# RWKV triangular inverses: from whole 64x64 blocks to 32x32 blocks with a corner, and where projection products stand

## The reference

```python
def step(s, inp):
    r_t, w_t, k_t, v_t, kk_t, a_t = inp
    sa = jnp.einsum('bhvk,bhk->bhv', s, -kk_t)
    s = (s * w_t[:, :, None, :] + sa[..., None] * (kk_t * a_t)[:, :, None, :]
         + v_t[..., None] * k_t[:, :, None, :])
    return s, jnp.einsum('bhvk,bhk->bhv', s, r_t)
```

## Time and profile before

| | us |
|---|---|
| median of 3 runs | 4723.03 |
| lowest and highest of them | 4722.28, 4724.2 |
| the profiled execution | 4724.49 |
| its span, first to last instruction | 4722.8 |

### The profile page before, as it was taken

One profiled execution on the slowest core, in us unless ns is written; L12 is line 12 of the kernel. 1 busy time (PEld: TensorE's weight loads), 2 busy tenths in 40 slices (PEclk: granted clock), 3 DMA queues, 4 the chain that ended last, 5 costly groups with the idle time before them and its releaser, 6 DMA issues. The chain is left out here.

```text
span 4722.8 us, 86694 instructions
## 1 busy us (share of the span) xinstructions
PE 4354.9 (92%) x40017; PEld 2726.9 (58%) x40017; DVE 1375.2 (29%) x2899; ACT 539.0 (11%) x1016; POOL 134.1 (3%) x253
## 2 busy tenths in 40 slices
PE   5899999999999999799999987999995999999995
PEld 2577768686868776677777764554442333333331
DVE  1133333424142524324444552110123111111112
ACT  1011212112111211200111000000010000000001
POOL 0000000000000000100000000000000000000000
PEclk7899999999999999899999988999997999999997
DMA  9111111111111111121122106875128999999997
GB/s 357 47 57 34 48 34 49 44 44 48 37 48 35 48 37 39 53 64 54 55 60 62 51 6 224 295 258 198 62 81 319 372 390 391 396 398 390 387 395 288
DMA packets 412717, 738.32 MB, mean 156 GB/s; under 512 B 16382, under 2 KB 255300, under 8 KB 389444
## 3 DMA queue, kind: packets, MB, share of 16 engines
q1 hardware_dynamic: 405060, 697.65, 41.1%
q0 software_dynamic: 7296, 35.13, 2.7%
HBM read 689.21 MB, written 43.52 MB: 155 GB/s over the span
## 5 line engine op out<-in xcount | busy, mean ns | idle before, releaser
L512 PE MATMUL psR<-hT,wrkv 128*128 128x320 f32 x3584 | 983.0, 435 | 16.5 <-DMA wrkv<-in_w_in 16.5
L512 PEld LDWEIGHTS psR<-hT,wrkv 128*128 128x128 f32 x3584 | 683.3, 191 | 300.7 <-DMA wrkv<-in_w_in 17.0
L992 PE MATMUL psH<-hT,whg 128*128 128x320 f32 x2560 | 706.2, 434 | 24.4 <-DMA whg<-in_w_in 24.4
L992 PEld LDWEIGHTS psH<-hT,whg 128*128 128x128 f32 x2560 | 482.7, 191 | 215.9 <-DMA whg<-in_w_in 24.9
L526 PE MATMUL psR<-X 64*64 64x64 f32 x8960 | 285.7, 220 | 8.3 <-ACT X L715 3.7
L1277 PE MATMUL psM<-branches,wmg 128*128 128x512 f32 x512 | 265.1, 600 | 23.9 <-DMA branches<-outr_scratch 22.7
L526 PEld LDWEIGHTS psR<-X 64*64 64x64 f32 x8960 | 271.8, 135 | 24.6 <-ACT X L715 9.7
L1451 PE MATMUL psO<-wout,mergedT 128*128 128x512 f32 x480 | 208.7, 597 | 6.3 <-DMA wout<-in_w_out 5.8
L822 DVE TENSOR_TENSOR X<-X,psR 128x256 f32<-128x256 f32 (+1 forms) x240 | 90.6, 377 | 382.3 <-PE psR L526 380.5
L1837 DVE SCALAR_TENSOR_TENSOR hid<-hid,psE 128x512 f32<-128x512 f32 x16 | 11.0, 688 | 586.9 <-ACT hid L1797 586.9
L1716 PE MATMUL psE<-hT,xg 128*32 128x512 f32 x1392 | 168.6, 603 | 3.2 <-DMA hT<-in_moe_w_gate 2.6
(11 more groups left out here) (345 smaller groups left out, 4726.5 us busy)
## 6 DMA issues: line engine op xcount, KB each, us to landing
hT<-in_ada_w SPq DMA_DIRECT2D x64, 1024.0 KB, 8.3
wrkv<-in_w_in SPq DMA_DIRECT2D x56, 1024.0 KB, 6.0
mergedT<-in_moe_w_down SPq DMA_DIRECT2D x46, 1024.0 KB, 20.9
hT<-in_moe_w_gate SPq DMA_DIRECT2D x45, 1024.0 KB, 19.0
wmore<-in_moe_w_up SPq DMA_DIRECT2D x44, 1024.0 KB, 21.1
hT<-in_moe_w_down SPq DMA_DIRECT2D x43, 1024.0 KB, 22.3
hT<-in_moe_w_up SPq DMA_DIRECT2D x42, 1024.0 KB, 19.2
mergedT<-in_moe_w_up SPq DMA_DIRECT2D x42, 1024.0 KB, 19.4
```

The costliest lines, as they stand in the source:

```text
L512: mm = nc.tensor.matmul(ps[:, 2 * (n % 2) + h, 0:HALF], w[:, n % SLOTS, k, :], S["hT"][:, k, h * HALF:(h + 1) * HALF], start=(k == 0), sto ...
L992: mm = nc.tensor.matmul(ps[:, b + h, 0:HALF], w[:, i, k, :], S["hT"][:, k, h * HALF:(h + 1) * HALF], start=(k == 0), stop=(k == KT - 1))
```

## The change

The inverse of a 64x64 triangular matrix is taken by 32x32 blocks. The two diagonal blocks of each head are inverted by the same doubling, in 5 levels, with four 32x32 matmuls (`blocks`) where two of 64x64 stood. The off-diagonal block is then one step: the off-diagonal block of N times one diagonal inverse, a turn of the other, a copy into YT, and a product (the corner). POOL and DVE put the blocks into a new tile TI, which the scan reads. The chunk groups of the inverse are two of 5 chunks (HALVES) in place of 4, 4 and 2, so a level has 4 units. G1 and G3 are still whole 64x64 grams; the diagonal blocks are taken out by quarters (32 partitions each): G1's by DVE with a mask, G3's by ACT, with the off-diagonal block (Noff), and POOL applies the mask to G3's. `fill(42)` ahead of the inverse and 48 of the `fill(52)` behind it move: four products behind each of the 20 units, five more behind the last unit, five behind the off-diagonal step; four remain ahead of the scan. ACT takes gate tiles 2 and 3 ahead of its copies of units 2 and 11. `make_masks` makes four 64-wide masks in place of six and three 32-wide ones (cd: two strict triangles of -1, and the identity).

The diff, cut to its core:

```diff
-        X = [sb(f"X{d}", [P, NCH, 3, L]) for d in both]
+        X = [sb(f"X{d}", [P, NCH, 3, BL]) for d in both]
+        Noff = [sb(f"Noff{d}", [P, NCH, BL]) for d in both]
+        TI = [sb(f"TI{d}", [P, NCH, L]) for d in both]
+        YT = X[0]
...
-        UNITS, LEV = len(GROUPS), 6
+        HALVES = ((0, 5), (5, 5))
+        UNITS, LEV = len(HALVES), 5
+        near = [[slice(L * h + BL * d, L * h + BL * d + BL) for h in range(2)] for d in both]
+        far = [near[1 - d] for d in both]
...
         def _(pool):
+            for d in both:
+                nc.gpsimd.memset(TI[d][:, :, :], 0.0).then_inc(sem("ti_zeroed"), 1)
+            pool.wait_ge(sem("ti_zeroed"), 2)
...
-                        pool.wait_ge(sem("m_ready"), (2 * r + d) * 3 + g + 1)
-                        nc.gpsimd.tensor_tensor(X[d][:, c0:c0 + n, 2, :], X[d][:, c0:c0 + n, 1, :], bcast(ci[:, :], n, 1), ALU.add)\
+                        pool.wait_ge(sem("m_ready"), 4 * ((2 * r + d) * 3 + g + 1))
+                        nc.gpsimd.tensor_tensor(X[d][:, c0:c0 + n, 2, :], X[d][:, c0:c0 + n, 1, :], bcast(cd[:, 2, :], n, 1), ALU.add)\
+                            .then_inc(sem("tt_begun"), 1)
+                        pool.wait_ge(sem("g3_taken"), 6 * ((2 * r + d) * 3 + g + 1))
+                        nc.gpsimd.tensor_tensor(X[d][:, c0:c0 + n, 0, :], X[d][:, c0:c0 + n, 0, :], bcast(cd[:, 1 - d, :], n, 1), ALU.mult)\
                             .then_inc(sem("tt_begun"), 1)
                 for i in range(2, 4):
                     store_gate(i)
+                pool.wait_ge(sem("inv_added"), INV * (r + 1))
+                for d in both:
+                    for i in range(4):
+                        q, at = slice(BL * i, BL * i + BL), BL * (i % 2)
+                        nc.gpsimd.tensor_copy(TI[d][q, :, at:at + BL], X[d][q, :, 2, :]).then_inc(sem("ti_diag"), 1)
...
+            def blocks(out, lhsT, rhs):
+                for i in range(4):
+                    q = slice(BL * i, BL * i + BL)
+                    mm = nc.tensor.matmul(out[q], lhsT[q], rhs[q], start=True, stop=True)
+                return mm
...
                 for i in range(LEV):
                     for d in both:
-                        for k, (c0, n) in enumerate(GROUPS):
+                        for k, (c0, n) in enumerate(HALVES):
                             q = (i * 2 + d) * UNITS + k
                             if q >= 2:
                                 W("inv_copied", inv_copied(r, q - 2))
                                 if inv_added(r, q - 2) > r * INV:
                                     W("inv_added", inv_added(r, q - 2))
+                            if i >= 2:
+                                W("inv_added", inv_added(r, q - 2 * UNITS))
                             for c in range(c0, c0 + n):
...
                                 if i < LEV - 1:
-                                    mm = heads(o[:, 0:L], M, N)
+                                    mm = blocks(o[:, 0:BL], M, N)
                                 if i < LEV - 2:
-                                    mm = heads(o[:, L:P], N, M)
+                                    mm = blocks(o[:, BL:L], N, M)
                                 if i:
-                                    mm = heads(t, N, TT)
+                                    mm = blocks(t, N, TT)
                             mm.then_inc(sem("inv_sums"), 1)
-
-            def scan(r):
+                            fill(4)
+                fill(5)
                 W("inv_copied", INV * (r + 1))
                 W("inv_added", INV * (r + 1))
+                for k, (c0, n) in enumerate(HALVES):
+                    y, t = cols(4 + 2 * k, n, BL), cols(5 + 2 * k, n, BL)
+                    for c in range(c0, c0 + n):
+                        for d in both:
+                            for h in range(2):
+                                nc.tensor.matmul(y[near[d][h], c - c0, :], Noff[d][far[d][h], c, :], X[d][far[d][h], c, 2, :],
+                                                 start=True, stop=True)
+                        for d in both:
+                            for h in range(2):
+                                mm = nc.tensor.matmul(t[near[d][h], c - c0, :], X[d][near[d][h], c, 2, :], cd[near[d][h], 2, :],
+                                                      start=True, stop=True)
+                    mm.then_inc(sem("far_sums"), 1)
+                fill(5)
+                W("far_taken", UNITS * (r + 1))
+                for c in range(NCH):
+                    mm = blocks(cols(6, NCH, BL)[:, c, :], YT[:, c, 1, :], YT[:, c, 0, :])
+                mm.then_inc(sem("corner"), 1)
+
+            def scan(r):
+                W("ti_diag", 8 * (r + 1))
+                W("ti_corner", 4 * (r + 1))
...
-                fill(42)
                 inverse(r)
-                fill(52)
+                fill(4)
                 scan(r)
...
+                        W("g3", (2 * r + d) * 3 + g + 1)
+                        for i in range(4):
+                            q, at = slice(BL * i, BL * i + BL), BL * (i % 2)
+                            A(X[d][q, c0:c0 + n, 0, :], cols(6, n, L)[q, :, at:at + BL], ACT.Copy).then_inc(sem("g3_taken"), 1)
+                        for q in far[d]:
+                            A(Noff[d][q, c0:c0 + n, :], cols(6, n, L)[q, :, BL * d:BL * d + BL], ACT.Copy, scale=-1.0)\
+                                .then_inc(sem("g3_taken"), 1)
-                for i in (2, 3):
-                    take_gate(r, i)
...
+                            if q == 2:
+                                take_gate(r, 2)
+                            if q == 11:
+                                take_gate(r, 3)
...
+                for k, (c0, n) in enumerate(HALVES):
+                    W("far_sums", UNITS * r + k + 1)
+                    A(YT[:, c0:c0 + n, 0:2, :], ps[:, 4 + 2 * k:6 + 2 * k, 0:n * BL].rearrange("p g (c l) -> p c g l", c=n), ACT.Copy)\
+                        .then_inc(sem("far_taken"), 1)
...
-                        V.tensor_tensor(X[d][:, cs, 1, :], G1[:, :, 0:L], mask(mNT), ALU.mult).then_inc(sem("m_ready"), 1)
+                        for i in range(4):
+                            p, at = slice(BL * i, BL * i + BL), BL * (i % 2)
+                            V.tensor_tensor(X[d][p, cs, 1, :], cols(4, n, P)[p, :, at:at + BL], bcast(cd[p, d], n, 1), ALU.mult)\
+                                .then_inc(sem("m_ready"), 1)
...
-                        W("g3", u + 1)
-                        V.tensor_tensor(X[d][:, cs, 0, :], G3, mask(mN), ALU.mult).then_inc(sem("g3_taken"), 1)
...
+                W("corner", r + 1)
+                for d in both:
+                    for q in near[d]:
+                        V.tensor_copy(TI[d][q, :, BL * (1 - d):BL * (1 - d) + BL], cols(6, NCH, BL)[q]).then_inc(sem("ti_corner"), 1)
```

More of the change, by code:

```diff
@@ L23 @@
 NCH = T // L
+BL = L // 2
 HG_HEADS = 8
@@ L301, in make_masks @@
     link(nc.gpsimd.memset(cm[:, :, :], 1.0))
-    link(nc.gpsimd.memset(cm[:, 0, :], -1.0))
-    link(nc.gpsimd.memset(cm[:, 2, :], -1.0))
     for h in range(2):
         q = slice(L * h, L * h + L)
[L306 to L311, removed]
+        sel(cm[q, 0, :], ALU.is_ge, 0, [[1, L]], -1)
+        sel(cm[q, 1, :], ALU.is_ge, 0, [[-1, L]], 1)
+        sel(cm[q, 2, :], ALU.is_gt, 0, [[1, L]], -1)
+        sel(cm[q, 3, :], ALU.is_gt, 0, [[-1, L]], 1)
+    cd = C["cd"]
+    link(nc.gpsimd.memset(cd[:, 0:2, :], -1.0))
+    link(nc.gpsimd.memset(cd[:, 2, :], 0.0))
+    for i in range(4):
+        q = slice(BL * i, BL * i + BL)
+        sel(cd[q, 0, :], ALU.is_gt, 0, [[1, BL]], -1)
+        sel(cd[q, 1, :], ALU.is_gt, 0, [[-1, BL]], 1)
+        link(nc.gpsimd.affine_select(out=cd[q, 2, :], in_=cd[q, 2, :], compare_op=ALU.not_equal, fill=1.0, base=0,
+                                     pattern=[[-1, BL]], channel_multiplier=1))
     link(nc.gpsimd.memset(C["ci"][:, :], 0.0))
@@ L555, in inverse @@
                 last = 6 * (r + 1)
-                W("g1_taken", 2 * last)
+                W("g1_taken", 5 * last)
                 W("g2_taken", 2 * last)
-                W("g3_taken", last)
+                W("g3_taken", 6 * last)
                 W("bk_taken", last)
-                W("tt_begun", last)
+                W("tt_begun", 2 * last)
                 for i in range(LEV):
                     for d in both:
-                        for k, (c0, n) in enumerate(GROUPS):
+                        for k, (c0, n) in enumerate(HALVES):
                             q = (i * 2 + d) * UNITS + k
@@ L608, in scan @@
                         W(f"nr_ready{d}", 10 * r + j + 1)
-                        heads(Sa[d], X[d][:, order[d][j], 2, :], nR[d], start=False, part=True).then_inc(sem(f"sa_sums{d}"), 1)
+                        heads(Sa[d], TI[d][:, order[d][j], :], nR[d], start=False, part=True).then_inc(sem(f"sa_sums{d}"), 1)
                     for d in both:
@@ L800, in _ @@
                         cs = slice(c0, c0 + n)
[L801 removed]
```

(10 more changed lines are left out.)

28 lines of the change are left out of this document (12 added, 16 removed).

## The result

The changed kernel takes 4765.39 us (median of 4 runs, 4760.18 to 4767.29) against 4723.61 for the kernel before beside it (4 runs, 4722.28 to 4727.85): a ratio of 1.0085, interval 1.0068 to 1.0103. It is 0.85% slower. Forecast were 4651 and a range up to 4730. The profiled execution took 4760.18 us, its span is 4758.5.

What follows compares the result with a forecast made beforehand. PE was taken to bound each round: 15.8 + 7.5 + 4.3 = 27.6 us against 37.2, 9.6 less, 67 in seven rounds plus 7 in the last, 74 off, giving 4651 us; range 4617 to 4730.

Steps and rivals of the forecast that it cites:

- the prices of what PE does: Inverse, per round: 2,000 small records at 7.9 ns, 15.8 us; 22 blocks of fill at 0.34 us, 7.5 us.
- Rival A: Units of the inverse: the four row tiles do not run at once, 4778 or 4961 us, slower; chance 0.17.
- Rival C: Fill between units: the switch from 32-row tiles is dear, 0.7 us a block, 4711 us; chance 0.07.
- 25 ns a matmul: Units of the inverse: estimate from the skill's some 60 cycles a matmul, 50 us a round, landing in Rival A.
- What bounds the kernel now: RWKV round: one PE stream, shortened only by less PE work, lengthened by every PE wait; 37.2 us beside fill records.
- 27.5 ns as the densest record stream in the trace: Small matmuls: router-stage record spacing, taken as the upper bound on the price, 55 us a round.
- Moved or behind other work, at nothing: Round: moved gate copies and stores, weight tiles issued in the same order, clearings and mask making cost nothing.
- the bare evictions: Grams to inverse: PE waits for uncovered copies and the first tile switch, 4.3 us a round, bounds 1.5 to 6.9.
- Rival B: Grams: ACT's quarter copies each cost their full 0.28 us, 6.9 in place of 4.3 us, 4672 us; chance 0.13.
- The last round: Last round, only 36 products behind its grams: 30.7 us against 37.5, so 7 less.
- POOL's block copies: Before the scan: eight copies take 6.9 us, covered by about 12; without cover, in the last round, they end last.
- What would show it: Signs of being wrong: records at 13 ns or more, PE waiting inside units, or for POOL before the scan every round.

Runs made afterwards that it cites:

- Experiment 1: Changed kernel, but every weight tile from the fourth on loaded with 1 of its 16 slices (64 KB for 1 MB); 4713.52 us, ratio 0.9973 to the kernel before.
- the second split of experiment 7: Weight tiles loaded in four 256 KB parts, no wait for the last part or at the tile ahead of lw; changed kernel 4737.9 us, with experiment 6's mends 4638.5.
- Experiment 2: Changed kernel with ACT's six quarter and off-diagonal copies ahead of the turned copy in each gram group; 4715.19 us, ratio 0.998 to the kernel before.
- experiments 6: Changed kernel with ACT's quarters first, products sharing weights joined in levels 1 and 2, eight fill products moved ahead of the inverse; 4643.88 us, ratio 0.9831.
- experiment 4: Changed kernel with no fill between the units: 42 products ahead of the inverse, 42 behind the last unit; 4891.97 us, ratio 1.0352 to the kernel before.

## Why the prediction was wrong

*Right:* the prices of what PE does. 8.3 ns a record for 7.9 and 0.35 us a block for 0.34, so Rival A as I put it (tiles that don't overlap) and Rival C are out. The case that came stood in none of the rivals. The Trainium skill, TensorEngine Tiling (Array Packing), Restrictions and Gotchas, says that different row tiles cannot access one PSUM bank at the same time; by that the four tiles would take turns at 32 ns a record. The trace does not agree: four on the diagonal, each into its own 32 partitions of one bank, run at 8.3. Nor does it agree with the 25 ns a matmul that was estimated from the same page's Instruction Overhead.

*The step that failed* is "What bounds the kernel now": that a round is one PE stream, which only PE's work or a wait for another engine's data lengthens. PE's instructions are a third supply. I had the row in hand, "27.5 ns as the densest record stream in the trace", and read it as a bound on what the array does. The packets give about the same, 3.7 us for 128 records or 29 ns, but that row could not show it: its 26 records are less than one packet, and a quarter of the 111 ns worked out for one tile accounts for them. The inverse before used 29 ns a record, just inside; the new one uses 8.3, and lives on what the fill between lets arrive. The cost was 5.3 us of breaks a round, put at nothing. The Trainium skill, Advanced Engine Details and Errata, ISA Cache, has lines of 16 KB with 256 instructions; the trace agrees (6.06 MB in 370 packets). How often one comes, only the runs show.

*With it failed* "Moved or behind other work, at nothing: SP issues the same weight tiles in the same order". The order is the same, but the tiles used to load beside dense fill (one began at its end), which needs a packet in 34 us (128 x 0.2692), and now load beside units that need one in 3.5. Experiment 1 and the second split of experiment 7 show that this makes the long breaks.

*Mis-sized:* the bare evictions, 7.4 for 4.3. It is Rival B (6.9): quarters that each take their whole time, as ACT's rows show. Experiment 2 shows that most was order, not work.

*Not in the sum:* the half clock behind PE's waits, 3.4 us a round. The rows of before show 1.00 in the round's windows, and I did not ask what the clock does where PE stands for 2.45 or 3.1 us. That each such stretch in the units follows a stand of PE is shown (17 of 17 in the trace of the changed kernel), and the one behind the wait ahead of the inverse goes when that wait goes or gets shorter (experiments 6 and 2).

*The last round:* 14.6 us more for 7 less, so 21.6 off. From 1933.36 to 1955.44, where no fill is left, 840 records take 22.1 us, and at 8.3 ns they would take 7.0: 15.1 of the 21.6, from packets and half clock together. The bare evictions are 3.1 more (7.4 for 4.3). The sum also had POOL's block copies end last, at 6.9 us; they took 4.0, and DVE's corner copies ended last, as the off-diagonal step and the corner stood for instructions too (1.1 and 1.6 us).

"What would show it" named PE waiting inside the units as a sign of being wrong. It is there, but no other engine's data are what it waits for.

## What to carry to other kernels

Before making matmuls smaller, divide the instructions of the stretch by the time they will take and hold that against the instruction queue: here 256 of them per 3.7 us, some 29 ns for a load and a matmul. Here small tiles paid once dense work of few instructions stood between them, products that share weights were joined and the evictions were in the right order. Cutting large loads in parts helped where instructions were short (27.5 us on the changed kernel), and by no more than the noise where they were not; SP's waits for the parts must not stand ahead of an urgent load. An eviction split in four is four evictions, so the piece that is waited for goes first.

## What was not expected of the hardware

- PE's instructions come in 16 KB packets over the DMA engines, one per 3.7 us on the mean of eleven steps in experiment 4, and 232 pairs were in stock after 22.9 us of fill. A 1 MB load held the next packet up by about 3 us (due near 358.4 by the pace before it, started at 361.4). PE goes on 1.2 to 1.6 us after a packet has landed (97 breaks of experiment 4).
- Four 32x32 tiles on the diagonal, all writing one PSUM bank, run a float32 record of 32 columns in 8.3 ns.
- An ACT copy of 32 partitions and 128 elements takes 0.29 us in a row of four, with no overlap.
